# Reordering TensorE's work: a projection tile in front of the retention scores, transposes between the products of a feed-forward end

## The reference

```python
# layer 0
h = x @ w_in                       # q, k, v, gate of 4 retention heads (128 wide), q, k, v of 8 stick-breaking heads (64 wide)
ret = retention(rotary(rq), rotary(rk), rv)     # scores * decay, times v, per head
ret = silu(rg) * (ret - mu) * rsqrt(var + eps)  # norm over the head's 128 values
sb = stick_breaking(sq, sk, sv)
m = concat([ret, sb]) @ w_out
x = layer_norm(ALPHA * x + m)
# feed-forward, once in each of the two layers
h = x @ w_up                       # 1024 -> 2 x 2816
h = causal convolution of 3 taps along the tokens
f = (silu(g) * u) @ w_down         # 2816 -> 1024
x = layer_norm(ALPHA * x + f)
```

## Time and profile before

| | |
|---|---|
| device time, median of 3 executions | 2378.58 us (2376.06 to 2378.64) |
| the profiled execution | 2379.54 us, span 2377.9 us, mean granted clock 0.944 |
| busy, share of the span | PE 2141.3 us (90%), DVE 1358.9 (57%), ACT 1089.2 (46%), POOL 202.2 (9%) |
| PE instruction groups around the change | scores L348, projections L319 and L511/L517, down products L1016, transposes L808 |
| POOL's loads for the small stages | issued from 1.49 to 20.74 us |
| retention, from the first projection to the third stick projection | 21.38 to 183.49 us |
| end of feed-forward 0: last down product ends, next block's first product starts | 736.15, 758.42 us |
| end of feed-forward 1: the same | 1411.1, 1444.0 us |
| expert stage: first weight load issued | 1778.6 us |

### The profile page before, as it was taken

How to read it: one execution, slowest core, us unless ns; L and a number is a source line. 1 busy time by engine, 2 the same in 40 slices (tenths; PEclk the granted TensorE clock), 3 DMA queues, 4 the chain that set the end, 5 groups by cost and what they waited for, 6 DMA issues and landing times. The chain is left out here.

```text
span 2377.9 us, 27922 instructions
## 1 busy us (share of the span) xinstructions
PE 2141.3 (90%) x10028; PEld 1707.4 (72%) x10028; DVE 1358.9 (57%) x1792; ACT 1089.2 (46%) x1200; POOL 202.2 (9%) x238
## 2 busy tenths in 40 slices
PE   7889989999997999699999977899946999999993
PEld 5767668888885777488888865686435888777773
DVE  3441247555435455566555356666135988888885
ACT  3324534343322445424343224364205888777773
POOL 1000110000001000100000000000010222222222
PEclk9989999999998999699999998899957999999996
DMA  7123026742332221233333223210108999999995
GB/s 216 54 69 100 18 71 245 228 111 84 111 94 76 63 63 63 71 91 95 101 94 103 93 53 81 73 70 1 48 31 294 399 399 399 398 398 398 399 399 202
DMA packets 275687, 377.84 MB, mean 159 GB/s; under 512 B 12748, under 2 KB 174732, under 8 KB 275464
## 3 DMA queue, kind: packets, MB, share of 16 engines
q1 hardware_dynamic: 258248, 315.14, 39.5%
q0 software_dynamic: 17344, 61.41, 6.9%
HBM read 340.30 MB, written 38.84 MB: 159 GB/s over the span
## 5 line engine op out<-in xcount | busy, mean ns | idle before, releaser
L980 PE MATMUL PS<-XS,split 128*128 128x512 f32 (+1 forms) x2304 | 482.3, 371 | 3.6 <-DVE XS L153 3.1
L980 PEld LDWEIGHTS PS<-XS,split 128*128 128x128 f32 x2304 | 406.4, 188 | 79.3 <-DVE XS L153 3.6
L153 DVE TENSOR_TENSOR moe_split<-moe_raw,moe_split 128x2048 fp32r<-128x2048 f32 x174 | 398.0, 2289 | 86.0 <-ACT moe_split L148 85.8
L153 DVE TENSOR_TENSOR split<-ring,split 128x2048 fp32r<-128x2048 f32 x111 | 254.1, 2292 | 293.6 <-ACT split L148 293.4
L148 ACT CAST moe_split<-moe_raw 128x2048 fp32r<-128x2048 f32 x174 | 332.6, 1913 | 70.0 <-DMA moe_raw<-in_expert_w_gate 38.3
L2511 PE MATMUL PS<-moe_split,moe_x 128*128 128x512 f32 x1392 | 347.7, 400 | 8.0 <-DVE moe_split L153 4.8
L2511 PEld LDWEIGHTS PS<-moe_split,moe_x 128*128 128x128 f32 x1392 | 258.9, 190 | 71.6 <-DVE moe_x L153 12.6
L148 ACT CAST split<-ring 128x2048 fp32r<-128x2048 f32 x112 | 213.1, 1904 | 200.5 <-PE PS L1016 110.8
L1016 PE MATMUL PS<-split,XS 128*128 128x512 f32 x960 | 218.5, 389 | 0.3 <-DVE XS L153 0.3
L1016 PEld LDWEIGHTS PS<-split,XS 128*128 128x128 f32 x960 | 180.0, 188 | 38.4 <-issue 1.1
L2533 PE MATMUL PS<-moe_split,moe_h 128*128 128x512 f32 x696 | 167.1, 396 | 2.1 <-DVE moe_h L153 2.1
(11 more groups left out here) (347 smaller groups left out, 2454.2 us busy)
## 6 DMA issues: line engine op xcount, KB each, us to landing
moe_raw<-in_expert_w_gate SPq DMA_DIRECT2D x58, 1024.0 KB, 13.8
moe_raw<-in_expert_w_up SPq DMA_DIRECT2D x58, 1024.0 KB
moe_raw<-in_expert_w_down SPq DMA_DIRECT2D x58, 1024.0 KB, 13.0
ring<-in_w_up SPq DMA_DIRECT2D x88, 512.0 KB, 5.2
ring<-in_w_down SPq DMA_DIRECT2D x44, 512.0 KB, 4.4
expert_rows<-rows POOLq DMA_DIRECT2D x4, 4096.0 KB, 30.4
expert_rows<-W POOLq DMA_DIRECT2D x29, 512.0 KB, 7.0
ring<-in_w_in SPq DMA_DIRECT2D x24, 512.0 KB, 5.3
```

Of the source, the lines that this page charges most:

```text
L153: return dve.tensor_tensor(lo, raw, hi.bitcast(F32), ALU.subtract)
L980: mm = pe.matmul(PS[:, b + q, rows], w[:, c, q, :], x_half(k, high)[:, c, rows], start=(c == 0 and m == 0), stop=(c == KC - 1 and m == 2))
```

## The change

Four edits, of which the last only makes room.

1. In retention, tile 0 of the next head is projected between the turning of q and k and the scores; tile 1 stays behind the scores.
2. In the last head the small stages' PE work takes the place of that tile, the stick stage's projections 0 and 1 (now `k.stick_project`) stand behind the scores and behind the products with v, and ACT makes the two small copies behind the copies of q and k. The stick stage then starts with projections 2 and 3. The stages' other functions keep their places.
3. In both feed-forward ends `tail.turn(pe, t - 1)` stands behind the products of tile t, and `turn(3)` at the end.
4. The halves of the last three pieces of h go to a new buffer `HX`, which lies over the raw h of pieces 0 to 5 in `W`, instead of to `XS`, which the tail now fills while those products run. Writing them waits for the low halves of the pieces that lay there.

```diff
@@ retention_stage, tensor
                 mm.then_inc(qk_turned, 1)
+            if h + 1 < H:
+                project(h + 1, 0)
+            else:
+                for small in k.small_tensor:
+                    small(pe)
             pe.wait_ge(qk_out, 2 * h + 2)
...
             if h + 1 < H:
-                project(h + 1, 0)
                 project(h + 1, 1)
+            else:
+                k.stick_project(pe, 0)
             pe.wait_ge(masked, 4 * h + 4)
...
                 project(h + 1, 2)
                 project(h + 1, 3)
+            else:
+                k.stick_project(pe, 1)
             turn_y(h)
@@ retention_stage, scalar
                 act.copy([qT, kT][part], PS[:, part, :]).then_inc(qk_out, 1)
+            if h + 1 == H:
+                for small in k.small_scalar:
+                    small(act)
             piece_high(k, act, 2 * h + 4)
@@ stick_stage
+    def project(pe, u):
+        n, what, which = turns[u]
+        if u >= 2:
+            pe.wait_ge(kept, u - 1)
+        elif u == 0:
+            pe.wait_ge(k.ret_kept, 16)
+            pe.wait_ge(k.ret_rotated, 16)
+            pe.wait_ge(k.cols_in, 1)
+            pe.wait_ge(k.taps_in, 1)
...
+    k.stick_project = project
+
     def tensor(pe):
...
-        pe.wait_ge(k.cols_in, 1)
-        pe.wait_ge(k.taps_in, 1)
-        for u in range(4):
-            project(u)
+        for u in (2, 3):
+            project(pe, u)
         pe.wait_ge(k.bias_masked, 1)
@@ ffn_stage
-        return k.H0[:, high, :] if p == 0 else k.XS[:, high, (p - 1) % 4 * 1024:(p - 1) % 4 * 1024 + 1024]
+        if p == 0:
+            return k.H0[:, high, :]
+        if p >= UD - SPLIT:
+            return k.HX[:, p - (UD - SPLIT), high, :]
+        return k.XS[:, high, (p - 1) % 4 * 1024:(p - 1) % 4 * 1024 + 1024]
...
-            act.wait_ge(split_used, AHEAD + 2 * UD + max(p - 4 + 1, 0))
+            if p < UD - SPLIT:
+                act.wait_ge(split_used, AHEAD + 2 * UD + max(p - 4 + 1, 0))
+            else:
+                act.wait_ge(h_low, 2 * (p - (UD - SPLIT)) + 1 + 2)
...
             mm.then_inc(tail.product, 1)
-        pe.wait_ge(tail.summed, 1)
-        for t in range(NT):
-            tail.turn(pe, t)
+            if t > 0:
+                tail.turn(pe, t - 1)
+        tail.turn(pe, NT - 1)
@@ program
+                nc.sbuf_tensor("HX", [P, SPLIT, 2, 1024], F32R) as HX, \
...
-            yield taps_stage(k)
-            yield column_stage(k)
-            bias = bias_stage(k)
-            yield bias
+            taps, cols, bias = taps_stage(k), column_stage(k), bias_stage(k)
+            k.small_tensor = [taps["tensor"], cols["tensor"], bias["tensor"]]
+            k.small_scalar = [taps["scalar"], cols["scalar"]]
+            yield dict(gpsimd=taps["gpsimd"])
+            yield dict(gpsimd=cols["gpsimd"])
+            yield dict(gpsimd=bias["gpsimd"], scalar=bias["scalar"], vector=bias["vector"])
```

More of the change, by code:

```diff
@@ L494, in sync @@
                 load_slab(k, sp, k.pieces[n], [columns(w, 2048 + p * P + 512 * part, P) for part in range(2)])
-    def tensor(pe):
[L497 to L518, removed]
-                                           start=(c == 0 and m == 0), stop=(c == KC - 1 and m == 2))
-            mm.then_inc(projected, 1)
-            if u % 2 == 1:
-                piece_done(k, pe.drain(), n)
-        pe.wait_ge(k.cols_in, 1)
-        pe.wait_ge(k.taps_in, 1)
-        for u in range(4):
-            project(u)
@@ new lines, in project @@
+    def project(pe, u):
[7 more added lines that the diff above has]
+            pe.wait_ge(k.taps_in, 1)
+        bank = 6 + u % 2
+        piece_ready(k, pe, n)
+        wh, wl = piece_halves(k, n, KC)
+        if what != "v":
+            part = slice(P, 2 * P) if what == "k" else slice(0, P)
+            for c in range(KC):
+                for m, (w, high) in enumerate(((wh, 1), (wh, 0), (wl, 1))):
+                    mm = pe.matmul(PS[:, bank, :], w[:, c, part], x_half(k, high)[:, c, :],
+                                   start=(c == 0 and m == 0), stop=(c == KC - 1 and m == 2))
+        else:
+            for t in (2 * which, 2 * which + 1):
+                for c in range(KC):
+                    for m, (high, w) in enumerate(((1, wh), (1, wl), (0, wh))):
+                        mm = pe.matmul(PS[:, bank, 256 * (t % 2):256 * (t % 2) + 256],
+                                       x_half(k, high)[:, c, t * P:(t + 1) * P], w[:, c, :],
+                                       start=(c == 0 and m == 0), stop=(c == KC - 1 and m == 2))
+        mm.then_inc(projected, 1)
+        if u % 2 == 1:
+            piece_done(k, pe.drain(), n)
@@ L2805, in program @@
                 nc.sbuf_tensor("XS", [P, 2, KC * S], F32R) as XS, \
-                nc.sbuf_tensor("W_head", [P, 14080], F32), \
+                nc.sbuf_tensor("HX", [P, SPLIT, 2, 1024], F32R) as HX, \
+                nc.sbuf_tensor("W_rest", [P, 14080 - SPLIT * 2048], F32), \
                 nc.sbuf_tensor("H0", [P, 2, 1024], F32R) as H0:
-            k.split, k.XS, k.H0 = split, XS, H0
+            k.split, k.XS, k.HX, k.H0 = split, XS, HX, H0
         with nc.sbuf_tensor("moe_raw", [P, 6, SLOT], F32) as moe_raw, \
```

## The result

The changed kernel took 2340.31 us, median of 4 runs (2336.80 to 2344.57), beside 2378.61 us for the kernel before (4 runs, 2376.06 to 2381.18). The ratio is 0.9838, 95% interval 0.9823 to 0.9854, so 38.3 us less. Measured a second time it took 2337.0 us (5 runs, 2336.32 to 2343.17) beside 2378.9: 0.983 (0.9817 to 0.9844), 41.9 us less by the medians. The forecast was 2337, with 2330 to 2348. The profiled run of the changed kernel, the fastest of its four, took 2336.8 us (span 2335.2, mean granted clock 0.952 instead of 0.944).

The account below looks back on a forecast made before the run. PE, busy 90% of the span, was taken as the bound, with idle stretches paid again as half clock. Gains of 10.3+11.9+6.6+12.4 = 41.2 us off the 2378.6 median gave 2337 us, eight in ten between 2330 and 2348.

Parts of the forecast that it names:

- Heads 0 to 2: Retention: projecting the next head's tile before the scores removes idle time and regains full clock, gaining 10.3 us.
- Rival (a): Retention: the clock isn't regained, heads give 5.3 us and the last about 7, time 2347; chance 0.17.
- The last head: Retention's end up to the third stick projection: small stages and projections fill PE's waits, gaining 11.9 us, bounds 6 and 13.
- the wait before V: Before the third stick projection: PE idles 2.8 us until ACT's queued copies free bank 6.
- rival (d): Stick stage: idle time before the third projection leaves PE at half clock, making the kernel slower, 2355 to 2425; chance 0.02.
- Feed-forward 0: First feed-forward end: last tile's norm starts 9.8 us sooner, less 3.2 for POOL holding DVE; gain 6.6 us.
- the hold of line 859 by POOL: First feed-forward end: POOL's subtraction delays DVE's two-SBUF-operand instruction in the last tile's norm, costing 3.2 us.
- Rival (b): POOL doesn't hold line 859 and the stalls on piece 2h+3 vanish: 3.2+2.1 us more, 2332; chance 0.12.
- Feed-forward 1: Second feed-forward end: a new 1 us wait, DVE keeps up with PE, last tile's norm starts sooner; gain 12.4 us.
- Rival (e): A feed-forward end: ACT's order still holds the square root back, 19 us less gain, 2356; chance 0.02.
- The sum: Whole kernel: gains of 10.3, 11.9, 6.6 and 12.4 us make 41.2, giving 2337 us.
- rival (c): Behind a block end or in the stick stage: an unseen wait takes back about 12 us, 2349; chance 0.07.

## Why the prediction was right, step by step

**Heads 0 to 2:** 10.3 us predicted, 10.8 measured (29.86, 29.90 and 29.94 us from one head's transposes to the next, instead of 32.88, 33.32 and 34.34). The stall was foretold at 0.7 and is 0.72 to 0.74; the clock is regained, and the run with useless products shows its share: 5.8 us of clock and so 5.1 of idle time, where the sum had 5.0 and 5.3. Rival (a) is out for these heads.

**The last head** is the term that was mis-sized. Up to V, 11.9 us were predicted. Five executions of this order gave 10.8 us where its scores took 4.02 us, 12.4 in three where they took 2.42, and 9.7 where they took 4.63. That spread is the clock's, and the prediction had no term for it. The mechanism was seen rightly (the wait before V, 2.8 predicted, 2.67 measured, with the four ACT instructions named). The step that failed is the price of this wait: I charged it as idle time only, and kept the clock behind it for rival (d), as a state that lasts through the stage. In truth V ran at 1.2 GHz for 3 to 6 us, at its beginning, and then at full clock. From V to the first stick scores it took 13.5 to 14.8 us instead of 12.1, so 1.4 to 2.7 us go back, and the last head gives 8.1 to 11.0 us (9.2 in the first trace), not 11.9. I had the row for it: the pair behind the 4.20 us of idle time took 13.17 instead of 11.17 us, 2 us. Rival (d) is out as a state that lasts. Its two times were also added up wrongly: by its own rule, 60 and 130 us more on top of 2337 are 2397 and 2467 us; 2355 and 2425 take the gain off twice.

**Feed-forward 0:** 6.6 predicted, 6.5 measured in the marks. It rested on the hold of line 859 by POOL, costed at 3.2 from rows of other instructions; L872 took 3.3 longer, and keeping POOL away made that vanish. Rival (b) is out as to the hold. But removing the hold doesn't bring its 3.2 us, since the next block then waits for POOL: of the two ways tried one lost 0.5 us and the other gained 1.0.

**Feed-forward 1:** 12.4 predicted, 12.2 measured (from the first down product, 1290.97 before and 1261.82 after, to the hybrid block); the new wait was put at 1 us and is 0.94, and DVE kept up. Rival (e) is out.

**The sum** was 41.2 us. Its four terms measured 10.8, 9.2, 6.5 and 12.2 us in the first trace, together 38.7, and 39.3 in the second of the same kernel; what is missing against 41.2 is in the last head. The profiled executions stand 42.7 us apart, nearer to the forecast, but 1.6 of these arise before the change, 1.0 in the odd block and 1.4 net behind the hybrid block's start; that part of the agreement is luck. The medians give 38.3 and 41.9. They differ by 3.3 us for one kernel: its runs spread over 8 us (2336.3 to 2344.6), those of before over 6. The varying clock is seen in the traces and is a part of that; that it is all of it isn't shown. Of rival (c) only the 1.4 to 2.7 us in V were there.

## What to carry to other kernels

Work that needs nothing of the waiting result belongs into the wait, and on TensorE it can pay twice: here, in three heads, 5.1 us of idle time and 5.8 us of clock. So charge a new gap with its idle time and with the products behind it at 1.2 GHz (here 1.3 to 2.7 us for a gap of 2.7), and look for it in the order of the engine that releases it: here ACT had a table load in front of the copy that mattered. Expect this part to vary from run to run. When a POOL instruction and a DVE instruction with two operands in SBUF meet on the path, try cutting the POOL one in pieces before you put it behind (here 1.0 us gained against 0.5 lost), and see which engine the end of the block waits for.

## What the runs showed of the hardware

- A DVE SCALAR_TENSOR_TENSOR on two SBUF operands that met a POOL subtraction took 4.58 instead of 1.28 us and ended 1.08 us after it. With the subtraction in quarters two DVE instructions took 1.35 and 2.04 us, and the quarters 6.91 us together instead of 4.50. The same DVE operation with one operand in PSUM took 1.27 us in the midst of POOL's subtraction.
- At the end of this block the next one's first product came 3.81 to 3.82 us after the end of POOL's last instruction in the four kernels that move or cut POOL's work, and 1.31 us after DVE's in the kernel before and the changed one, where POOL had ended some 6 us before DVE.
- Eleven useless products in each of four gaps of 2.1 to 2.6 us made the kernel 8.4 us faster: the granted clock stayed at 1.00, and four score products took 2.3 to 2.4 us instead of 3.5 to 4.6.
- Behind one and the same gap of 0.52 us, four score products took 4.02 us in one execution and 2.42 in others, and in one they took 4.63 us with no gap in front; behind 2.7 us, 96 products of V took from 13.0 to 14.4 us.
